# VectorE's evictions ahead of the ranks, and two expert pairs' rows kept on the chip, in a decoder layer with sparse attention and 32 experts

## The chip, the cores and the metric

The program runs on one core of a Trainium2 chip. The metric is the device time of one execution in microseconds (us), lower is better. Everything is float32; the large projections outside the experts run as three passes over operands split into a rounded part and its rest.

## The reference, cut to what matters

One layer over 512 tokens of width 1024: a projection, sparse attention beside causal pooling, an output projection, a layer norm, and then a layer of experts with a second layer norm. Only the last part matters here:

```python
pg_top, g = lax.top_k(softmax(t @ w_r1 + b_r1), 1)          # one of 4 groups
pe, e_local = lax.top_k(softmax((t @ w_r2 + b_r2)[group g]), 2)   # two of its 8 experts
weights = pg_top * pe / sum(pe)
for e in range(32):
    a = silu(t @ w_gate[e]) * (t @ w_up[e])                 # 1024 -> 256
    y = y + combine[:, e:e + 1] * (a @ w_down[e])           # 256 -> 1024
out = layer_norm(ALPHA * t + y)
```

Each token goes to two of the 32 experts. One expert's weights are 3 MB, all of them 96 MB, and each is read once.

## The kernel before, in words

**Up to the router.** The 512 tokens are 4 tiles of 128. For each tile TensorE (PE) makes the output projection, VectorE (DVE) adds the residual and takes the statistics, ScalarE (ACT) normalises, PE transposes the normalised rows (`transpose_h`, L1377), ACT evicts four of the eight 128x128 blocks (L829) and DVE the other four (`transposed_h`, L1048), and PE multiplies them with the router's weights (`router`, L1386). Meanwhile GpSimd (POOL) scales the tile with the norm's gain and offset (L683, L684), and SyncE (SP) stores it to `h_rows` in HBM. DVE's `route` (L1055 to L1078) finds the group and the two experts of each token.

**Ranks and lists.** A token's place among those of its expert is a rank: PE multiplies a triangle with the one-hot rows (`ranks`, L1408, L1409), DVE's `place` (L1102 to L1111) turns the ranks of several tiles into one-hot rows over 64 places (`at_rank`, L1107), and PE multiplies these with the token numbers (`lists`, L1416). Tiles 0 to 2 are ranked together, and tile 3 by itself once its `route` is done. DVE's order of work is as it is written in the code: `place` for tiles 0 to 2, `transposed_h(3)`, `route(3)`, `place` for tile 3, the lists (`row_from`, L1122).

**The pairs.** Two experts of 64 places each make a pair, 16 pairs in all (p = 0 to 15, `LAST` = 15). POOL gathers a pair's 128 rows from HBM (`gather`, L698, into `xe`), PE transposes them (`rows`, L1446), PE multiplies with gate and up weights (`gate_up`, L1460, 32 matmuls), ACT and DVE make the activation (L852, L1129), PE transposes it (L1471) and multiplies with the down weights (`down`, L1484, 16 matmuls). DVE and ACT evict the halves of the result into `ye` (`y_out`, L1135, L865), one buffer, and POOL scatters the rows to `y_rows` in HBM (`store_y`, L705), for pairs 0 to 14. An eviction of pair p waits until the store of p-1 has landed. The weights go through six slots, three pairs' worth. SP issues all of them on its one queue: a pair's gate and up weights when the pair three before is through `gate_up`, its down weights when that pair is through `down`.

**The end.** When pair 13 is through `down`, SP loads gain and offset of the second norm (`g2`, `b2`, L549, L550). Then it waits until all 15 stores have landed and reads `y_rows` back in eight loads of 512 KB, two for each tile (`yg`, L563). Between them stands a branch for the case that an expert has more than 64 tokens (L554, not taken here). Pair 15 is not stored: DVE builds for each tile of tokens a matrix of weights (`place_w`, L1170, 8 instructions, after pair 13), PE transposes it (L1539) ahead of pair 15's `gate_up`, ACT evicts it (`placeT`, L902), and PE multiplies it with pair 15's rows (L1548, 8 products of two instructions), so that the rows come out at their tokens. On DVE the end is `add_stored(0)` (two instructions, L1209), `gated(15)` (L1129), `add_stored(1)`, `add_stored(2)`, `y_out(15)`, `add_stored(3)`, and then for each tile `add_last` (L1216 to L1220) and `finish` (L1225, L1226).

Of the kernel before, what the change touches and what calls it, by code (L numbers as in the profile page):

```python
# [30 lines left out]
ALU = mybir.AluOpType  # L31
# [3 lines left out]
P = 128  # L35
# [25 lines left out]
LAST = PAIRS - 1  # L61
PAIR_SLOTS = ((2, 3), (1, 0), (4, 5))
# [26 lines left out]
def layer_kernel(nc, x, w_in, w_pool, pool_scale, w_out, rel_bias, ln1_g, ln1_b, w_r1, b_r1, w_r2, b_r2,  # L89
                 w_gate, w_up, w_down, ln2_g, ln2_b, onehot, headfix, out):  # L90
    ctx = ExitStack()
    with ctx:
# [13 lines left out]
        for j in range(SLOTS):  # L106
# [38 lines left out]
        place_w = at("place_w", SLOT + 20 * KB, [NT, 2, CAP])  # L145
        placeT = at("placeT", SLOT + 22 * KB, [NT, P])
# [20 lines left out]
        ye = at("ye", o, [D])  # L167
# [7 lines left out]
                   [at("x_again1_0", o + 4 * KB, [D // 2]), at("x_again1_1", o + 10 * KB, [D // 2])]]  # L175
        sil = [at(f"sil{i}", o + 4 * KB + KB * i, [DE]) for i in range(2)]
# [68 lines left out]
        last_rank, last_wt = at("last_rank", wpool_at, [2, NT, 2]), at("last_wt", wpool_at + 64, [2, NT, 2])  # L245
        row_sum, neg_mean = at("row_sum", wpool_at + 128, [NT, 2]), at("neg_mean", wpool_at + 160, [NT])
        square_sum, std2, rstd2 = [at(name, wpool_at + 192 + 32 * i, [NT]) for i, name in enumerate(("square_sum", "std2", "rstd2"))]
# [119 lines left out]
        y_stored = sem("y_stored")  # L367
# [72 lines left out]
        LAST_BANKS = ((0, 1), (2, 3), (6, 7), (4, 5))  # L440
# [5 lines left out]
        def _(sp):  # L446
# [104 lines left out]

            sp.wait_ge(y_ps, 2 * LAST)
# [6 lines left out]

            sp.wait_ge(y_stored, 16 * LAST)  # L560
            for t in range(NT):
                for c in range(2):
                    sp.dma_start(yg[t][c][:, :], y_dram[SEQ * c + P * t:SEQ * c + P * t + P, :]).then_inc(y_gathered[t], 16)  # L563
# [9 lines left out]
        def _(pool):  # L573
# [128 lines left out]
            def store_y(p):  # L702
                pool.wait_ge(y_lo, p + 1)
                pool.wait_ge(y_hi, p + 1)
                pool.indirect_dma_start(out=y_dram, out_offset=bass.IndirectOffsetOnAxis(ap=row_to[:, p:p + 1], axis=0),  # L705
                                        in_=ye[:, :], in_offset=None,
                                        bounds_check=2 * SEQ - 1, oob_is_err=False).then_inc(y_stored, 16)
# [5 lines left out]
            for p in range(LAST):  # L713
                if p + 3 < PAIRS:
                    gather(p + 3)
                store_y(p)
# [3 lines left out]
        def _(act):  # L720
# [140 lines left out]
            def y_out(p):  # L861
                act.wait_ge(y_ps, 2 * p + 2)
                if p:
                    act.wait_ge(y_stored, 16 * p)
                act.activation(ye[:, 512:], bank[5][:, :], ACT.Copy).then_inc(y_hi, 1)  # L865
# [15 lines left out]
            for p in range(LAST - 1):  # L881
                rows_out(p + 2)
                silu(p + 1)
                y_out(p)
                act_out(p + 1)
            y_out(LAST - 1)

# [13 lines left out]
            act.wait_ge(placeT_ps, 1)  # L901
            act.activation(placeT[:, :, :], bank[0][:, :].rearrange("p (t s) -> p t s", t=NT), ACT.Copy).then_inc(placeT_ready, 1)  # L902
            silu(LAST)
            act_out(LAST)
            y_out(LAST)
            for t in range(NT):
# [7 lines left out]
        def _(dve):  # L914
# [216 lines left out]
            def y_out(p):  # L1131
                dve.wait_ge(y_ps, 2 * p + 1)
                if p:
                    dve.wait_ge(y_stored, 16 * p)
                dve.tensor_copy(ye[:, 0:512], bank[4][:, :]).then_inc(y_lo, 1)  # L1135
# [21 lines left out]
            for c in range(2):  # L1157
                link(dve.tensor_tensor(last_rank[:, c, :, :], hot[:, :, c, NE - 2:NE], rk[:, :, c:c + 1].to_broadcast([P, NT, 2]), ALU.mult))
                link(dve.tensor_tensor(last_wt[:, c, :, :], hot[:, :, c, NE - 2:NE], wt[:, :, c:c + 1].to_broadcast([P, NT, 2]), ALU.mult))
# [3 lines left out]
            for p in range(LAST - 1):  # L1163
                rows_out(p + 2)
                gated(p + 1)
                y_out(p)

            for t in range(NT):
                for e in range(2):
                    ins = dve.tensor_scalar(place_w[:, t, e, :], iota_r[:, :], last_rank[:, 0, t, e:e + 1], last_wt[:, 0, t, e:e + 1],  # L1170
                                            ALU.is_equal, ALU.mult)
            ins.then_inc(place_ready, 1)
# [71 lines left out]
        def _(pe):  # L1244
# [247 lines left out]
            for p in range(LAST - 1):  # L1492
                rows(p + 2)
                gate_up(p + 1)
                down(p)
                transpose_act(p + 1)
# [37 lines left out]

            pe.wait_ge(xeT_act, PAIRS)
            pe.wait_ge(xeT_dve, PAIRS)
            pe.wait_ge(place_ready, 1)
            for t in range(NT):
                ins = pe.transpose(bank[0][:, P * t:P * t + P], place_w[:, t, :, :].rearrange("p n s -> p (n s)"), ident[:, :])  # L1539
            ins.then_inc(placeT_ps, 1)  # L1540
# [3 lines left out]
            pe.wait_ge(placeT_ready, 1)  # L1544
            for t in range(NT):
                for c in range(2):
                    pe.wait_ge((y_lo, y_hi)[c], PAIRS)
                    pe.matmul(bank[LAST_BANKS[t][c]][:, :], placeT[:, t, :], ye[:, 512 * c:512 * c + 512], start=True, stop=True).then_inc(last_ps, 1)  # L1548

# [25 lines left out]
```

## Time and profile before

| | us |
|---|---|
| the three runs | 616.8, 593.65, 613.6 |
| their median | 613.6 |
| the profiled execution | 593.69 |
| its span | 592.0 |
| PE busy | 499.4 (84%) |
| DVE busy | 229.1 (39%) |
| POOL busy | 161.9 (27%) |
| ACT busy | 149.7 (25%) |

The span runs from the first to the last instruction; 1.7 us of the profiled execution lie around it. Times within the trace are microseconds from the span's start. Busy shares are means over stages with different limits, so that a term is read from the waits of its own stage. A clock of 1.00 in the rows is TensorE at 2.4 GHz, 0.50 at 1.2 GHz. The profiled execution lies at the lowest of the three runs, 20 us below their median.

### The profile page before, as it was taken

Reading aid. Unit: us, or ns where it says so; the run is one execution under the profiler, and the core shown is the slowest. Engines: PE = TensorE matmul, PEld = TensorE weight load, DVE = VectorE, ACT = ScalarE, POOL = GpSimd, SP = SyncE. Lnnn points to the kernel's source line nnn. Section 1 sums busy time; section 2 is a strip of 40 time slices with the busy share of each in tenths; the row PEclk is TensorE's granted clock in tenths of the full one; section 3 lists DMA queues with packets and bytes.
Section 4 is the critical chain, followed back from the end, with each engine's and each line's share of the span. In section 5 each row is a group of like instructions: output and inputs, shape, how many; then the busy total and the mean of one; then the engine's idle time right before and its main releaser. Section 6 shows DMA issues by size and latency. Waiting matters only on the chain.

```text
span 592.0 us, 6141 instructions
## 1 busy us (share of the span) xinstructions
PE 499.4 (84%) x2182; PEld 283.7 (48%) x2182; DVE 229.1 (39%) x554; ACT 149.7 (25%) x311; POOL 161.9 (27%) x159
## 2 busy tenths in 40 slices
PE   5999999999799999999547799999786789777490
PEld 4586675856454556888443333333232333332130
DVE  2101482898789751255740211111111110102287
ACT  3233323522246664012410111111111111011032
POOL 2243332387624762033521011211111110101000
PEclk9999999999899999999757899999799998889875
DMA  9844458103029101990757799999999999998613
GB/s 321 298 50 51 51 164 259 38 1 142 1 92 356 52 1 37 389 389 38 276 222 270 303 396 418 422 417 419 421 421 419 422 419 419 422 420 329 237 78 142
DMA packets 42583, 148.29 MB, mean 251 GB/s; under 512 B 11362, under 2 KB 15970, under 8 KB 30264
## 3 DMA queue, kind: packets, MB, share of 16 engines
q1 hardware_dynamic: 37992, 139.71, 62.5%
q0 software_dynamic: 4464, 8.10, 3.7%
q8 instruction: 18, 0.29, 0.2%
q14 instruction: 13, 0.11, 0.1%
q10 hardware_dynamic: 96, 0.08, 0.0%
HBM read 137.16 MB, written 18.87 MB: 264 GB/s over the span
## 4 chain that ended last, share of the span: by engine, by line
PE 54%; DMA 20%; SPq 9%; DVE 7%; issue 5%; POOL 2%; ACT 2%; POOLq 0%; DVEq 0%; ACTq 0%
PE bank L1295 17%; DMA wgu<-in_w_up_dram 10%; PE bank L1460 8%; PE bank L1400 7%; DMA xe<-h_rows,row_from 6%; SPq L486 6%; PE bank L1268 3%; PE bank L1484 3%; PE bank L1362 3%; PE bank L1340 3%; SPq L489 3%; DMA y_rows<-ye,row_to 2%; PE bank L1315 2%; PE bank L1353 2%; PE bank L1446 1%
## 5 line engine op out<-in xcount | busy, mean ns | idle before, releaser
L1460 PE MATMUL bank<-wgu,xeT 128*64 128x512 f32 x512 | 127.9, 657 | 28.0 <-DMA wgu<-in_w_up_dram 27.2
L1460 PEld LDWEIGHTS bank<-wgu,xeT 128*64 128x64 f32 x512 | 42.6, 151 | 102.3 <-issue 100.1
L705 POOL DMA_INDIRECT y_rows<-ye,row_to x15 | 15.1, 1006 | 189.0 <-PE bank L1446 120.0
L1484 PE MATMUL bank<-wd,actT 128*64 128x512 f32 x256 | 60.7, 617 | 1.4 <-ACT actT L859 1.4
L1129 DVE TENSOR_TENSOR act_row<-bank,sil 128x256 f32<-128x256 f32 x16 | 6.8, 425 | 130.3 <-ACT sil L852 130.3
L607 POOL TENSOR_TENSOR ring_low<-ring,wt_high 128x1024 fp32r<-128x1024 f32 x12 | 28.6, 2384 | 55.4 <-ACT wt_high L732 55.4
L852 ACT ACTIVATE sil<-bank 128x256 f32<-128x256 f32 x16 | 6.1, 384 | 138.7 <-PE bank L1460 138.7
L1484 PEld LDWEIGHTS bank<-wd,actT 128*64 128x64 f32 x256 | 20.6, 142 | 37.6 <-issue 37.6
L1295 PE MATMUL bank<-xT_high,ring_low 128*128 128x512 f32 x128 | 32.7, 397 | 0.0
L1143 DVE COPY xeT<-bank 128x512 f32<-128x512 f32 x16 | 11.1, 692 | 54.6 <-PE bank L1446 54.6
L1340 PE MATMUL bank<-kT,qT 64*128 64x128 f32 (+3 forms) x64 | 26.0, 487 | 5.1 <-DVE nmx L995 4.3
L955 DVE SCALAR_TENSOR_TENSOR score<-relu,iw,score 128x256 f32<-128x256 f32 (+2 forms) x21 | 19.8, 942 | 26.2 <-ACT relu L775 26.0
L670 POOL TENSOR_SCALAR lg<-lg,rinv 128x128 f32<-128x128 f32 (+3 forms) x32 | 19.3, 603 | 34.8 <-DVE rinv L1025 34.8
L1295 PE MATMUL bank<-xT_high,wt_high 128*128 128x512 f32 (+1 forms) x104 | 28.1, 415 | 0.0
L937 DVE MAX8 m<-score 128x8 f32<-128x256 f32 (+2 forms) x48 | 26.9, 561 | 2.7 <-POOL score L641 1.6
L1295 PEld LDWEIGHTS bank<-xT_high,ring_low 128*128 128x128 f32 x128 | 23.4, 188 | 8.7 <-issue 3.6
L1295 PE MATMUL bank<-xT_low,wt_high 128*128 128x512 f32 (+1 forms) x104 | 27.3, 406 | 0.0
L1446 PE MATMUL bank<-ident,xe 128*128 128x128 f32 x128 | 19.4, 299 | 8.9 <-DMA xe<-h_rows,row_from 8.9
L1400 PE MATMUL bank<-wo_high,mix_high 128*128 128x512 f32 x64 | 25.5, 398 | 1.5 <-issue 1.5
L938 DVE MATCH_REPLACE8 score<-m,score 128x256 f32<-128x256 f32 (+2 forms) x48 | 26.1, 543 | 0.0
L1400 PE MATMUL bank<-wo_low,mix_high 128*128 128x512 f32 x64 | 25.0, 390 | 0.0
L1400 PE MATMUL bank<-wo_high,mix_low 128*128 128x512 f32 x64 | 24.9, 389 | 0.0
(202 smaller groups left out, 761.8 us busy)
## 6 DMA issues: line engine op xcount, KB each, us to landing
wgu<-in_w_gate_dram SPq DMA_DIRECT2D x32, 1024.0 KB, 23.2
wgu<-in_w_up_dram SPq DMA_DIRECT2D x32, 1024.0 KB, 27.7
wd<-in_w_down_dram SPq DMA_DIRECT2D x32, 1024.0 KB, 28.5
ring<-in_w_in_dram SPq DMA_DIRECT2D x5, 2048.0 KB, 13.1
wo<-in_w_out_dram SPq DMA_DIRECT2D x2, 2048.0 KB, 7.9
y_rows<-zero SPq DMA_DIRECT2D x1, 4096.0 KB, 21.8
yg<-y_rows SPq DMA_DIRECT2D x8, 512.0 KB, 6.6
bias_rows<-brow SPq DMA_DIRECT2D x1, 2560.0 KB
```

The source lines that it names most:

```text
L486: sp.dma_start(wgu[j][:, s, :, :], src[0, bass.ds(e, 1), :, :].rearrange("o (p k) f -> p (o k) f", p=P)).then_inc(loaded, 16)
L607: pool.tensor_tensor(low, raw, high.bitcast(F32), ALU.subtract).then_inc(wt_low_ready, 1)
L670: pool.tensor_scalar(p, p, rinv[:, u % 8:u % 8 + 1], 1.0, ALU.mult, ALU.mult).then_inc(prob_ready, 1)
L937: link(dve.max(m8[:, :], s_b))
L938: link(dve.match_replace(out=s_b, in_to_replace=m8[:, :], in_values=s_b, imm_value=TAKEN))
L955: ins = dve.scalar_tensor_tensor(out=s_b, in0=r, scalar=iw[:, b, j:j + 1], in1=s_b, op0=ALU.mult, op1=ALU.add)
L1295: ins = pe.matmul(bank[2 + i % 2][0:rows_out, :], lhsT, rhs, start=(s, k) == (0, 0), stop=(s, k) == (2, KD - 1))
L1340: pe.matmul(bank[qk_bank(u)][:, 0:keys(b)], qT[half(hh), hh // 2, P * b:P * b + P], kT[half(hh), hh // 2, 0:keys(b)], start=True, stop=Tru ...
L1400: ins = pe.matmul(bank[(2 if t % 2 == 0 else 0) + i][:, :], lhsT, rhs, start=(k, s) == (0, 0), stop=(k, s) == (KD - 1, 2))
L1446: ins = pe.transpose(bank[k // 4][:, P * (k % 4):P * (k % 4) + P], xv[:, k, :], ident[:, :])
L1460: ins = pe.matmul(bank[2 + i][half_rows(n), :], xeT[i][:, k, half_rows(n)], wgu[slots[n]][:, :, k, :], start=k == 0, stop=k == KD - 1)
L1484: ins = pe.matmul(bank[4 + c][half_rows(n), :], actT[i][:, m, half_rows(n)], wd[PAIR_SLOTS[p % 3][n]][:, m, 512 * c:512 * c + 512], start= ...
```

## The change

Two things are done.

1. In DVE's code `transposed_h(3)` stands ahead of `place` for tiles 0 to 2.
2. Pairs 14 and 15 (`KEPT` = 2) are both kept on the chip, and pairs 0 to 13 (`STORED` = 14) are stored. `ye` has two buffers, used in turn, each with its own semaphore, and an eviction waits for the store of two pairs before. The placing matrices for the two kept pairs are built in the loop's rounds 4 and 5 (`PLACE` = 4): DVE's 8 instructions at the round's start, PE's 4 transposes after `down`, into bank 6 or 7, and ACT's copy after its `act_out`. SP issues the eight `yg` loads ahead of the branch, when the stores of pairs 0 to 13 have landed. PE multiplies pair 14's rows for tiles 0 and 1 ahead of pair 15's `gate_up` and adds pair 15's to them afterwards; for tiles 2 and 3 both pairs' products come after `down(15)`. ACT computes one square root of one element after `y_out(15)`, which loads the table for it ahead of the norm's.

```diff
             sp.dma_start(b2[:, :], ln2_b[0].partition_broadcast(P)).then_inc(ln2_in, 16)
+            for i in range(2):
+                sp.wait_ge(y_stored[i], 16 * (STORED // 2))
+            for t in range(NT):
+                for c in range(2):
+                    sp.dma_start(yg[t][c][:, :], ...).then_inc(y_gathered[t], 16)
+
             sp.wait_ge(y_ps, 2 * LAST)
...
-            sp.wait_ge(y_stored, 16 * LAST)
-            for t in range(NT):
-                for c in range(2):
-                    sp.dma_start(yg[t][c][:, :], ...).then_inc(y_gathered[t], 16)
...
             def y_out(p):
                 dve.wait_ge(y_ps, 2 * p + 1)
-                if p:
-                    dve.wait_ge(y_stored, 16 * p)
-                dve.tensor_copy(ye[:, 0:512], bank[4][:, :]).then_inc(y_lo, 1)
+                if p >= 2:
+                    dve.wait_ge(y_stored[p % 2], 16 * (p // 2))
+                dve.tensor_copy(ye[p % 2][:, 0:512], bank[4][:, :]).then_inc(y_lo, 1)
...
+            transposed_h(NT - 1)
             dve.wait_ge(rank_ps, 1)
             place(0, NT - 1, bank[3][:, 0:NE * (NT - 1)])
-            transposed_h(NT - 1)
             route(NT - 1)
...
             for p in range(LAST - 1):
+                if 0 <= p - PLACE < KEPT:
+                    q = p - PLACE
+                    if q:
+                        dve.wait_ge(placeT_ps, q)
+                    for t in range(NT):
+                        for e in range(2):
+                            ins = dve.tensor_scalar(place_w[:, t, e, :], iota_r[:, :], ...)
+                    ins.then_inc(place_ready, 1)
                 rows_out(p + 2)
...
                 down(p)
+                if 0 <= p - PLACE < KEPT:
+                    pe.wait_ge(place_ready, p - PLACE + 1)
+                    for t in range(NT):
+                        ins = pe.transpose(bank[6 + p % 2][:, P * t:P * t + P], place_w[:, t, :, :]..., ident[:, :])
+                    ins.then_inc(placeT_ps, 1)
+                if 0 <= p - PLACE - 1 < KEPT:
+                    pe.wait_ge(placeT_ready, p - PLACE)
                 transpose_act(p + 1)
...
+            for t in range(2):
+                place_rows(t, STORED)
             gate_up(LAST)
             transpose_act(LAST)
             down(LAST)
+            for t in range(2):
+                place_rows(t, LAST)
+            for t in range(2, NT):
+                place_rows(t, STORED)
+                place_rows(t, LAST)
```

On DVE, between the router of tile 2 and that of tile 3, the order before is this (`hT_134` is the eviction of tile 3's transposes, `gl` the first instruction of `route(3)`):

```order
L1078 TENSOR_SCALAR neg<-em_191 128x1
L1102 SCALAR_TENSOR_TENSOR hot_rank<-bank,hot 128x3x32 x2
L1105 TENSOR_REDUCE rk<-hot_rank 128x6
L1107 TENSOR_TENSOR at_rank<-iota_r,rk 128x128 x3
L1111 TENSOR_TENSOR rank_219<-hot_rank 128x96
L1048 TENSOR_SCALAR hT_134<-bank,gT,bT 128x128 x4
L1055 TENSOR_TENSOR gl<-bank,br 128x4
```

The same place after the change:

```order
L1084 TENSOR_SCALAR neg<-em_192 128x1
L1054 TENSOR_SCALAR hT_132<-bank,gT,bT 128x128 x4
L1108 SCALAR_TENSOR_TENSOR hot_rank<-bank,hot 128x3x32 x2
L1111 TENSOR_REDUCE rk<-hot_rank 128x6
L1113 TENSOR_TENSOR at_rank<-iota_r,rk 128x128 x3
L1117 TENSOR_TENSOR rank_220<-hot_rank 128x96
L1061 TENSOR_TENSOR gl<-bank,br 128x4
```

The four evictions have moved ahead of the seven instructions of `place`; `route(3)` follows the last of these instead of the evictions.

On SP, at the program's end, the loads of `yg` stood behind the branch and ahead of the output's stores:

```order
L489 DMA wd_58<-in_w_down_dram 128x2048
L555 REGISTER_ALU
L555 COMPARE_AND_BRANCH
L554 UNCONDITIONAL_BRANCH
L563 DMA yg_0_100<-y_rows 128x1024
L563 DMA yg_1_101<-y_rows 128x1024
```

After the change they follow the norm's gain and offset directly:

```order
L492 DMA wd_56<-in_w_down_dram 128x2048
L552 DMA g_108<-in_ln_g_dram 128x1024
L553 DMA b_109<-in_ln_b_dram 128x1024
L559 DMA yg_0_100<-y_rows 128x1024
L559 DMA yg_1_101<-y_rows 128x1024
L559 DMA yg_0_102<-y_rows 128x1024
L559 DMA yg_1_103<-y_rows 128x1024
```

What has moved is the eight loads, past the wait for pair 14's `down` and past the branch. `wd_56` is the last load of expert weights, so nothing but gain and offset stands between the weights and `yg` on SP's queue.

## Rows read from the trace of the kernel before

**Rows 1.** The page: DMA busy tenths in 40 slices of 14.8 us.

```profile
DMA  9844458103029101990757799999999999998613
```

**Rows 2.** Windows: us, busy PE, PEld, DVE, ACT, POOL, clock, DMA share, GB/s.

```profile
304.00:309.00 5.00, 2.10 (x14) 1.89 (x14) 3.07 (x18) 2.06 (x5) 0.00 (x0) 0.50 0.00 0
520.00:535.00 15.00, 11.20 (x46) 4.38 (x48) 1.78 (x4) 0.53 (x2) 1.01 (x1) 0.89 1.01 419
549.00:553.00 4.00, 4.00 (x22) 1.41 (x18) 0.00 (x0) 0.00 (x0) 0.00 (x0) 1.00 0.13 45
```

**Rows 3.** Chain that ended last, 289 to 352 us: start, us, what.

```profile
289.57 1.98 PE bank L1377 x8
...
293.09 5.43 issue
298.52 3.62 PE bank L1386 x16
...
308.29 0.18 DVE row_from L1122
...
309.42 4.20 DMA xe<-h_rows,row_from
...
344.25 7.02 PE bank L1460 x32
```

**Rows 4.** Timeline of DVE, 292 to 302 us.

```profile
292.54 0.42 DVE L1102 SCALAR_TENSOR_TENSOR hot_rank<-bank,hot 128x96 f32<-128x96 f32 x2 [0.77 <-PE bank L1409]
...
293.38 3.35 DVE L1107 TENSOR_TENSOR at_rank<-iota_r,rk 128x128 f32<-128x128 f32 x3
...
297.06 1.36 DVE L1048 TENSOR_SCALAR hT<-bank,gT,bT 128x128 f32<-128x128 f32 x4
```

**Rows 5.** The first three at_rank instructions: ns min/median/max, first and last start.

```profile
L1107 DVE TENSOR_TENSOR at_rank<-iota_r,rk x3: 277/803/2425, 293.4 to 294.3; 128x128 f32<-128x128 f32 x3
```

**Rows 6.** Timeline of POOL, 284 to 320 us.

```profile
294.12 2.47 POOL L684 TENSOR_TENSOR h<-h,b 128x1024 f32<-128x1024 f32 x1
```

**Rows 7.** Tile h_rows, its store issued by SP at 296 to 297 us.

```profile
DMA to landing us min/median/max: 5.5/5.5/5.5
```

**Rows 8.** Line L1170, which builds the placing matrices on DVE.

```profile
L1170 DVE TENSOR_SCALAR place_w<-iota_r,last_rank,last_wt x8: 306/315/317, 534.9 to 536.5; 128x64 f32<-128x64 f32 x8
```

**Rows 9.** Timeline of PE, 536 to 576 us.

```profile
540.76 0.66 PE L1539 MATMUL bank<-ident,place_w 128*128 128x128 f32 x4
...
544.83 8.67 PE L1460 MATMUL bank<-wgu,xeT 128*64 128x512 f32 x32 [3.41 <-DMA wgu<-in_w_up_dram]
...
569.23 7.13 PE L1548 MATMUL bank<-ye,placeT 128*128 128x512 f32 x16
```

**Rows 10.** Chain that ended last, 532 to 569 us.

```profile
532.58 3.45 PE bank L1484 x16
...
537.51 7.85 DMA y_rows<-ye,row_to
...
553.78 4.54 DMA yg<-y_rows
...
560.98 0.43 DVE act_row L1129
...
562.84 6.46 PE bank L1484 x16
```

**Rows 11.** Line L550: the second norm's offset, issued at 536.4 us.

```profile
DMA to landing us min/median/max: 16.5/16.5/16.5
```

**Rows 12.** Tile yg, the last two loads, issued at 556.6 and 557.1 us.

```profile
DMA to landing us min/median/max: 8.1/8.5/8.9
```

**Rows 13.** Timeline of DVE, 560 to 575 us.

```profile
561.32 5.24 DVE L1209 SCALAR_TENSOR_TENSOR h<-yg,wt,h 128x1024 f32<-128x1024 f32 x4
...
567.22 2.60 DVE L1209 SCALAR_TENSOR_TENSOR h<-yg,wt,h 128x1024 f32<-128x1024 f32 x2
570.53 0.69 DVE L1216 CUSTOM_DVE_ANT_0 h<-bank,h 128x512 f32<-128x512 f32 x1 [0.72 <-PE bank L1548]
```

More of the change, by code:

```diff
@@ L61 @@
 LAST = PAIRS - 1
+KEPT = 2
+STORED = PAIRS - KEPT
+PLACE = 4
 PAIR_SLOTS = ((2, 3), (1, 0), (4, 5))
@@ L166, in layer_kernel @@
         hT = [at(f"hT{i}", o + 4 * KB * i, [KD, P]) for i in range(2)]
-        ye = at("ye", o, [D])
+        ye = [at(f"ye{i}", o + 4 * KB * i, [D]) for i in range(2)]
         o += 8 * KB
@@ L244, in layer_kernel @@
         eps_t = small("eps_t", [1])
[L245 to L247 removed]
+        last_rank, last_wt = at("last_rank", wpool_at, [2, NT, 2 * KEPT]), at("last_wt", wpool_at + 128, [2, NT, 2 * KEPT])
+        row_sum, neg_mean = at("row_sum", wpool_at + 256, [NT, 2]), at("neg_mean", wpool_at + 288, [NT])
+        square_sum, std2, rstd2 = [at(name, wpool_at + 320 + 32 * i, [NT]) for i, name in enumerate(("square_sum", "std2", "rstd2"))]
         rank1 = small("rank1", [NT, NE])
@@ L366, in layer_kernel @@
         y_hi = sem("y_hi")
-        y_stored = sem("y_stored")
+        y_stored = [sem(f"y_stored{i}") for i in range(2)]
         y_gathered = [sem(f"y_gathered{t}") for t in range(NT)]
@@ L712, in _ @@
             pool.wait_ge(y_zeroed, 16)
-            for p in range(LAST):
+            for p in range(STORED):
                 if p + 3 < PAIRS:
@@ L862, in y_out @@
                 act.wait_ge(y_ps, 2 * p + 2)
-                if p:
-                    act.wait_ge(y_stored, 16 * p)
-                act.activation(ye[:, 512:], bank[5][:, :], ACT.Copy).then_inc(y_hi, 1)
+                if p >= 2:
+                    act.wait_ge(y_stored[p % 2], 16 * (p // 2))
+                act.activation(ye[p % 2][:, 512:], bank[5][:, :], ACT.Copy).then_inc(y_hi, 1)
             for t in range(NT):
@@ L885, in _ @@
                 act_out(p + 1)
+                if 0 <= p - PLACE < KEPT:
+                    act.wait_ge(placeT_ps, p - PLACE + 1)
+                    act.activation(placeT[:, p - PLACE, :, :], bank[6 + p % 2][:, :].rearrange("p (t s) -> p t s", t=NT), ACT.Copy).then_inc(placeT_ready, 1)
             y_out(LAST - 1)
@@ L905, in _ @@
             y_out(LAST)
+            act.activation(probe[:, :], eps_t[:, :], ACT.Sqrt)
             for t in range(NT):
@@ L1166, in _ @@
                 y_out(p)
[L1168 to L1172, printed above, removed]
             y_out(LAST - 1)
@@ L1533, in _, with place_rows @@
                         ins.then_inc(o_y_ps, 1)
+                pe.wait_ge(o_added, NE * NT + 1)
+            def place_rows(t, p):
+                for c in range(2):
+                    pe.wait_ge((y_lo, y_hi)[c], p + 1)
+                    ins = pe.matmul(bank[LAST_BANKS[t][c]][:, :], placeT[:, p - STORED, t, :], ye[p % 2][:, 512 * c:512 * c + 512],
+                                    start=p == STORED, stop=p == LAST)
+                    if p == LAST:
+                        ins.then_inc(last_ps, 1)
             pe.wait_ge(xeT_act, PAIRS)
             pe.wait_ge(xeT_dve, PAIRS)
[L1537 to L1540, printed above, removed]
+            for t in range(2):
+                place_rows(t, STORED)
             gate_up(LAST)
```

29 lines of the change are left out of this document (13 added, 16 removed).

## The prediction, made before the changed kernel ran

> **What bounds the kernel now.** I read the page's slices first: the DMA engines are at nine tenths or more in an unbroken run of slices from the 24th to the 36th, 340 to 533 us, with an idle patch before it and a falling tail behind [rows 1]. The windows say the same in numbers: share 1.01 and 419 GB/s in 520 to 535 us, nothing at all in 304 to 309 us, and 0.13 in 549 to 553 us [rows 2]. So the expert stage is as long as its weights take, and what can be won lies before it, where nothing streams because the first gather isn't out, and behind it. The chain of waits, read in order of time, names both places: in the first, the router of tile 3 and the lists [rows 3]; in the second, pair 13's store, the first loads of `yg`, and pair 15's last matmuls [rows 10]. The timelines of single engines then tell what stands in each wait [rows 4 to 6, 9, 13].
>
> **Part 1, the eviction of tile 3 ahead of the ranks.** PE ends tile 3's transposes at 289.57 + 1.98 = 291.55 us. ACT's half follows at once: its eviction ends where the chain's 5.43 us of "issue" begin, at 293.09. DVE's half comes only after `place`, at 297.06 to 298.42 [rows 4], and the router starts at 298.52 [rows 3]. Now DVE evicts first. It is free at about 291.8 (the end of tile 2's route, just before its wait for the ranks ended at 292.54 [rows 4]), so with 1.36 us the eviction ends at 293.2, beside ACT's. The router runs 293.3 to 296.9, with the same 3.62 us.
>
> `route(3)`, which started when the router ended (298.52 + 3.62 = 302.14), now has two things to wait for: the router at 296.9, and `place`, which has moved behind the eviction. `place` starts at 293.2, and `at_rank` 0.84 us later (293.38 less 292.54 [rows 4]), at 294.0. Its three instructions took 277, 803 and 2425 ns [rows 5]: the third started at 294.3, under POOL's addition of 294.12 to 296.59 [rows 6], and ended right behind it. I take it that what is left of `at_rank` is held until 296.59 again, then takes two times 0.28 us, and 0.26 us of `rank` follows: 297.5. So `route(3)` starts at 297.6 and wins 302.1 - 297.6 = **4.5 us**. Bounds: 5.3 us if nothing is held and the router alone decides (302.1 - 296.9); 3.6 us if the three take their whole 3.35 us again from 294.0 with a wait of a microsecond behind. A loss is excluded: POOL's addition ends at 296.6 whatever DVE does.
>
> The Trainium skill (GPSIMD Engine Reference, Specifications) states that GpSimd shares SBUF interfaces with VectorE and that DVE instructions with two SBUF inputs contend for them. This case's trace agrees: 2425 ns against 277 for one shape. By the rule the term is 4.5 us, without it 5.3 us; the evictions, which read PSUM, keep their 1.36 us by it.
>
> Does the 4.5 us reach the end? The lists' last step moves from 308.5 to 304.0, and the gather needs `h_rows` as well: tile 3's store is issued when POOL's addition ends, at 296.6, and lands 5.5 us later, at 302.1 [rows 7]. That is 1.9 us early, so it doesn't decide. The next weights wait for the first gather, and the DMA engines are empty meanwhile [rows 2]; from the gather on [rows 3] every load is issued in a fixed chain behind it. The idle patch is cut by what is won, and the saturated stage of equal bytes moves as a whole. I count all 4.5 us.
>
> **Part 2, the placing work in rounds 4 and 5.** In each of the two rounds 8 instructions of 0.31 us on DVE, 2.5 us [rows 8], 4 transposes of together 0.66 us on PE [rows 9] and one copy on ACT; one such set goes at the end. I cost it at nothing. Its cover is the stream: PE runs ahead of it at this point, since three pairs were loaded early, and later waits for each pair's weights (3.41 us for the last [rows 9]). Without the cover a round would cost its 2.5 + 0.66 us, plus the price of a `gate_up` after a stall: 8.67 us against 7.02 us without one [rows 3, 9].
>
> **Part 3, the end.** Gone: pair 14's store (its issue on POOL and its landing), and the wait of `y_out(14)` for pair 13's store. PE's four products for pair 14 go in front of pair 15's `gate_up`. Eight such products took 7.13 us [rows 9], four take 3.6, from 541.4 (540.76 + 0.66) to 545.0, where PE waited for weights until 544.83 [rows 9]. Cost at most 0.2 us, and hidden, as shown below. They also keep PE at work, so `gate_up(15)` may run at 2.4 GHz throughout, 7.0 instead of 8.67 us.
>
> What matters is when `yg` for tile 0 has landed, since on DVE `add_stored(0)` stands ahead of `gated(15)`, and PE stood still from 553.5 until that was done, at 561.4 [rows 10]. Before, the loads were issued when pair 14's store had landed, 0.4 us ahead of the chain's 553.78, and tile 0 landed at 558.3, 4.9 us after that issue [rows 10]. Now they are issued when pair 13's store has landed, 537.51 + 7.85 = 545.4. Taken alone that is 8 us earlier. But the DMA engines aren't empty then. The norm's offset, the last thing on SP's queue ahead of `yg`, was issued at 536.4 and landed only at 552.9, 16.5 us later [rows 11], while the mean share had fallen to 0.13 [rows 2]: a few of the 16 engines still worked off weights when the others had nothing to do. A load is spread over all 16 and has landed with the slowest. So tile 0's `yg` ends behind the offset on the slowest engine: 552.9 plus two loads' shares. In the kernel before the second of the eight loads landed at 558.3 and the eighth at 566.0 (557.1 + 8.9 [rows 12]), 1.3 us apart, so 552.9 + 2.6 = 555.5. The term is 558.3 - 555.5 = **2.8 us**. Bounds: 1.6 us if the slow engine keeps the pace of its last two loads (3.8 us for the pair); 8.6 us if it doesn't hold up `yg` at all (next part).
>
> Behind that, all goes as before and 2.8 us earlier: PE has stood still, so `down(15)` takes its 6.46 us again, against 3.45 us for the same work in pair 13 [rows 10], as at half the clock [rows 10]; `add_stored(1)`, `(2)`, `y_out(15)` and `add_stored(3)` take 5.24 + 0.7 (567.22 less 566.56) + 2.6 us on DVE [rows 13] beside it. Four products come on top for tiles 2 and 3, 3.6 us, but DVE works from 570.5 to the end of the span on the four tiles, 5 us a tile, while PE was through at 576.4 [rows 9, 13]: hidden. The square root's table isn't on the path, since DVE first uses its result after the second tile's `add_last`.
>
> The Trainium skill (DMA: Bandwidth & Descriptors, Queues, rings and completion order) says that each DMA engine consumes the descriptors of a queue in ring order. That speaks against the early issue, and the offset's 16.5 us agree. By the rule the term is 2.8 us, without it 8.6 us.
>
> **Sum.** 593.7 - 4.5 - 2.8 = **586.4 us** for an execution like the profiled one. That one is the lowest of those shown, the median is 613.6 us, 20 us above, and nothing in the profile tells where these 20 us lie; I take the difference as the same there: 613.6 - 7.3 = **606.3 us**, 1.2% less.
>
> **The rivals.**
> *The loads aren't held up.* If `yg` for tile 0 lands 4.9 us after its issue as before, at 550.3 in the trace's time, `add_stored(0)` is done at 552.9. `gate_up(15)`, without a fall of the clock, ends at 552.0, so `gated(15)` runs at 552.9, `down` stays at 2.4 GHz (3.45 instead of 6.46 us [rows 10]), and DVE's own work decides: 553.3 + 5.2 + 0.7 + 2.6 = 561.9 instead of 570.5 [rows 13]. That is 8.6 us, with part 1 13.1 us: 580.6, at the median 600.5 us. For it: the bytes left at 549 us are few [rows 2]. Against: the offset's landing.
> *The stream swallows part 1.* If some DMA engines are so far behind that they never run dry between 304 and 340 us, the last weights come no earlier: only 2.8 us are left, 590.9, at the median 610.8 us. Against: the share is 0.00 for 5 us [rows 2].
> *Rounds 4 and 5 cost time: slower.* DVE builds the matrices ahead of `rows_out`, and PE waits for them between `down` and the next transposes. If PE decides there, each round costs 2.5 + 0.66 + 1.65 us (the last for the clock), 9.6 us for both, less the 7.3: 596.0, at the median 615.9 us, 2.3 us slower than before. For it: PE is nearly fully busy in this part of the stage. Against: the stream is saturated to 535 us [rows 2], and DVE's work fits while PE ends `down`. It decides from the point where the DMA share falls below 1 after these rounds.
>
> **How the numbers follow.** Forecast 0.60, loads not held up 0.18, part 1 swallowed 0.12, rounds cost time 0.10. The range must hold executions like the lowest and like the highest of those shown: down to 593.7 - 5.3 - 8.6 = 579.8, up to 616.8 - 3.6 - 1.6 = 611.6 us: 580 to 612. Two per cent, about what a measurement of this kernel can tell from no change, are 12 us. Only the first rival reaches that (13.1), so faster by more than 2% is 0.19 with a little for scatter; slower by more than 2% is 0.04, for scatter; within 2% 0.77.
>
> **What would show it.** Right: the router of tile 3 starting near 293.3 and the first gather 4.5 us earlier; the last `gate_up`'s weights at about 540.3; `yg` for tile 0 landing some 10 us after its issue, not 5; DMA share 1.0 through rounds 4 and 5. Wrong: `at_rank` ending after 298.5; pair 15's `down` at 3.5 us; a gap in the DMA share around pairs 4 to 7; tile 0's `yg` waited for by nobody.

## The result, and the profile after

| | before | after |
|---|---|---|
| the runs of this comparison, us | 616.8, 593.65, 613.6, 594.0 | 584.9, 584.92, 607.5, 586.08 |
| median | 603.8 | 585.5 |
| profiled execution | 593.69 | 584.9 |
| its span | 592.0 | 583.1 |

The ratio is 0.9865, with an interval of 0.9835 to 0.9895: 8 us less of 594. It isn't the ratio of the medians, because some executions of either kernel are 20 us longer (in the traces of e1_order and e11_twelve below, which are such executions, the granted clock is 0.50 from 200 to 240 us, where the profile after has 1.00), and the ratio leaves these out. The forecast was 7.3 us less, 586.4 for an execution like the profiled one. The changed kernel run once more gave 0.9864.

The page's slices (14.6 us each) answer to [rows 1]:

```profile
DMA  9944468004019200892487799999999999999803
```

The unbroken run of nines goes from 335 to 539 us, where it went from 340 to 533. The tail behind it was 8, 6 and 1 tenths, then 3 for the output's stores. Now it is 8 and 0, then 3: the eight `yg` loads fill the slice right behind the weights, where a few engines used to work alone.

Three windows of the changed kernel, with the columns of [rows 2]. The second holds PE's and ACT's placing work of rounds 4 and 5 and DVE's of round 5, the third is the stage behind it:

```profile
298.00:303.00 5.00, 2.11 (x14) 1.89 (x14) 3.28 (x19) 2.06 (x5) 0.00 (x0) 0.50 1.00 418
388.00:404.00 16.00, 15.56 (x84) 6.91 (x80) 4.14 (x12) 4.10 (x9) 2.82 (x3) 1.00 1.02 419
404.00:420.00 16.00, 14.49 (x72) 5.71 (x72) 2.50 (x4) 2.16 (x5) 3.27 (x4) 1.00 1.02 421
```

Before, 5 us ahead of the first gather had share 0.00 [rows 2]; now the early loads of weights run until 303, and the gather is issued at 303.69. Of the idle patch ahead of the gather some 0.7 us are left. Behind the gather a second one stands as before, where the next weights wait for `gate_up`: share 0.00 in 338 to 340 us before, in 332 to 334 us after. Through the placing rounds the share stays above 1.

The chain of waits of the changed kernel, 291 to 308 us (start, us, what), answers to [rows 3]:

```profile
291.16 1.36 DVE hT L1054 x4
292.53 0.34 DVE hot_rank L1108 x2
292.89 0.36 DVE rk L1111
293.28 2.86 DVE at_rank L1113 x3
...
296.27 0.26 DVE rank L1117
296.53 0.08 DVE gl L1061
...
302.57 0.19 DVE row_from L1128
...
303.69 4.45 DMA xe<-h_rows,row_from
```

The 5.43 us of "issue" and PE's router are gone from it. DVE evicts, makes the ranks and goes straight into `route(3)`. `row_from` stands at 302.57 instead of 308.29, 5.72 us earlier. Of that, 0.83 us were won before this place: tile 3's transposes start at 288.74 against 289.57, and nothing that the change touches lies ahead of them. It is scatter: in e12_again, the same kernel once more, they start at 290.18. So part 1 gave 4.9 us. From tile 3's transposes to `row_from` it is 18.72 us before and 18.71 in e2_kept, which has the old order; it is 13.83 us after and in e1_order and 13.82 in e12_again, which have the new one.

The three instructions that decide when `route(3)` starts are in the timelines of PE, of DVE's `at_rank` (ns min/median/max, first and last start) and of POOL:

```profile
292.63 3.60 PE L1395 MATMUL bank<-wr,hT 128*128 128x36 f32 x16 [0.96 <-ACT hT L833]
```

```profile
L1113 DVE TENSOR_TENSOR at_rank<-iota_r,rk x3: 279/293/2437, 293.3 to 295.8; 128x128 f32<-128x128 f32 x3
```

```profile
293.28 2.49 POOL L688 TENSOR_TENSOR h<-h,b 128x1024 f32<-128x1024 f32 x1
```

PE's wait is put down to ACT, but ACT's eviction is done at 292.25 and DVE's at 292.52, so DVE's is the one that releases the router, at 292.63. The router ends at 296.23 and `place` at 296.53, within 0.3 us. Again one `at_rank` takes 2.44 us beside POOL's addition, by itself in DVE's timeline:

```profile
293.49 2.44 DVE L1113 TENSOR_TENSOR at_rank<-iota_r,rk 128x128 f32<-128x128 f32 x1
```

This time it is the second: the first starts with the addition at 293.28 and takes its 0.29 us. The second ends at 295.93, 0.16 us behind the addition (295.77), and the third takes 0.28 us again.

The end, from the chain of waits of the changed kernel, answers to [rows 10]:

```profile
532.10 7.94 DMA y_rows<-ye,row_to
540.08 0.05 issue
540.13 0.33 SPq L559
540.46 0.04 issue
540.50 8.86 DMA yg<-y_rows
...
552.03 0.44 DVE act_row L1135
...
553.89 6.62 PE bank L1493 x16
```

And the offset's landing, which answers to [rows 11]; it was issued at 531.0:

```profile
DMA to landing us min/median/max: 15.8/15.8/15.8
```

`yg` is issued when pair 13's store has landed, and tile 0 lands at 549.36, 8.95 us earlier than before. The last weights that PE waits for, pair 15's up weights, came 5.33 us earlier (539.50 against 544.83), so part 2's and 3's own share is 3.6 us. It repeats: tile 0 lands 13.5 us behind these weights before and 13.6 in e1_order, and 9.9 after, 10.0 in e2_kept and 10.2 in e12_again, a share of 3.3 to 3.7 us.

PE's timeline, with the end of [rows 9]:

```profile
535.36 3.70 PE L1557 MATMUL bank<-ye,placeT 128*128 128x512 f32 x8
539.50 7.09 PE L1469 MATMUL bank<-wgu,xeT 128*64 128x512 f32 x32 [0.44 <-DMA wgu<-in_w_up_dram]
552.51 0.70 PE L1480 MATMUL bank<-ident,act_row 128*128 128x128 f32 x2 [5.92 <-DVE act_row L1135]
553.89 6.62 PE L1493 MATMUL bank<-wd,actT 128*64 128x512 f32 x16 [0.68 <-ACT actT L863]
560.44 10.57 PE L1557 MATMUL bank<-ye,placeT 128*128 128x512 f32 x24
```

Pair 14's four products end 0.44 us before the last weights are there and cost nothing. With PE at work until then, `gate_up(15)` takes 7.09 us instead of 8.67. That gain is worth nothing, since PE then waits 5.92 us for DVE, which waits for `yg`. `down(15)` is as slow as before, 6.62 us. The first `add_last` starts at 561.74 against 570.53 [rows 13].

### The profile page after: what moved, and what is told of

Same layout as the page of the kernel before. It is cut to its first block, busy times and chain, and to the rows that moved or that the text cites. A ratio compares the mean times of both kernels' runs of the same rounds, so it can differ in the third digit from the quotient of the medians.

```text
span 583.1 us, 6186 instructions
## 1 busy us (share of the span) xinstructions
PE 505.0 (87%) x2202; PEld 286.7 (49%) x2202; DVE 229.5 (39%) x562; ACT 150.5 (26%) x313; POOL 161.2 (28%) x158
## 4 chain that ended last, share of the span: by engine, by line
PE 54%; SPq 15%; DMA 13%; DVE 9%; issue 4%; POOL 2%; ACT 2%; POOLq 0%; DVEq 0%; ACTq 0%
PE bank L1304 17%; SPq L489 10%; PE bank L1469 8%; PE bank L1409 8%; DMA wgu<-in_w_up_dram 5%; SPq L492 5%; DMA xe<-h_rows,row_from 4%; PE bank L1493 3%; PE bank L1277 3%; PE bank L1371 3%; PE bank L1349 3%; PE bank L1324 2%; PE bank L1455 2%; PE bank L1362 2%; DMA yg<-y_rows 2%
## 5 line engine op out<-in xcount | busy, mean ns | idle before, releaser
L1469 PE MATMUL bank<-wgu,xeT 128*64 128x512 f32 x512 | 126.4, 650 | 23.3 <-DMA wgu<-in_w_up_dram 22.5
```

Of the source, the lines that this page charges most:

```text
L1469: ins = pe.matmul(bank[2 + i][half_rows(n), :], xeT[i][:, k, half_rows(n)], wgu[slots[n]][:, :, k, :], start=k == 0, stop=k == KD - 1)
```

## The experiments

Each kernel is compared with the kernel before on the same chip. "Of before" and "of after" say which kernel an edit starts from. Line numbers of edited kernels differ by one or two.

### The two halves by themselves

e1_order, of before:

```diff
+            transposed_h(NT - 1)
             dve.wait_ge(rank_ps, 1)
             place(0, NT - 1, bank[3][:, 0:NE * (NT - 1)])
-            transposed_h(NT - 1)
             route(NT - 1)
```

> The kernel before with part 1 alone: DVE evicts tile 3's transposes ahead of place for tiles 0 to 2. Theory: the 4.9 us that the two traces differ by between tile 3's transposes and the lists come from this alone, and the weights' stream behind it moves as a whole, so the last gate_up's weights land 4.9 us earlier and the time falls by 4.9 us (0.8%), from 593.7 to 588.8. The tail stays: tile 0's stored rows land 17 us after pair 15's last up weights are waited for, as before. Rival (the stream swallows it): the first gather comes 5 us earlier, but the last weights at the same time, 593.7.

Measured: 0.9917 (0.9903 to 0.9932), 4.9 us less. In its trace the distance from `row_from` to the last weights is 236.7 us, as it is before (236.5) and after (236.9). The stage isn't always as regular: it is 237.9 us in e12_again and 238.1 in e2_kept. So what is won ahead of the first gather passes through the streamed stage, to within this spread of 1.6 us; the ratio says the same with 0.9 us either way.

e2_kept, of after: the same lines put back into the order before, so that pairs 14 and 15 are kept and nothing else is changed.

> Part 2 alone: two kept pairs and early loads, the eviction back behind the ranks. Theory: only the tail gains, 3.6 us (what the stored rows of tile 0 came earlier by, counted from the last weights): 590.1 from 593.7. Place and route as in the kernel before (route of tile 3 starts 10.6 us after PE's transposes end). Rival (the two parts need each other, or rounds 4 and 5 cost something that part 1 hides): less than 2 us, 592 or more.

Measured: 0.9933 (0.9915 to 0.9952), 4.0 us less. The two halves add up to 8.9 us; the whole gave 8.0, known to 1.8 us either way: they are additive within what can be told. PE's timeline of this kernel:

```profile
540.20 3.70 PE L1557 MATMUL bank<-ye,placeT 128*128 128x512 f32 x8
545.97 8.78 PE L1469 MATMUL bank<-wgu,xeT 128*64 128x512 f32 x32 [2.06 <-DMA wgu<-in_w_up_dram]
```

Here a wait of 2.06 us was enough for a slow `gate_up(15)`, 8.78 us, where the changed kernel's 0.44 us left it at 7.09. The time of the whole doesn't show it.

### What holds up the yg loads

The prediction said that they queue behind the offset on the slowest DMA engines. A rival says that what counts is the ring that they stand in, so that another queue frees them; another that `yg` is slow by itself at this place.

e3_behind, of after, lets SP issue gain and offset behind `yg`:

```diff
-            sp.dma_start(g2[:, :], ln2_g[0].partition_broadcast(P)).then_inc(ln2_in, 16)
-            sp.dma_start(b2[:, :], ln2_b[0].partition_broadcast(P)).then_inc(ln2_in, 16)
-
...
             for t in range(NT):
                 for c in range(2):
                     sp.dma_start(yg[t][c][:, :], ...).then_inc(y_gathered[t], 16)
+            sp.dma_start(g2[:, :], ln2_g[0].partition_broadcast(P)).then_inc(ln2_in, 16)
+            sp.dma_start(b2[:, :], ln2_b[0].partition_broadcast(P)).then_inc(ln2_in, 16)
```

> The changed kernel with the loads of the second norm's gain and offset (g2, b2) behind the eight yg loads on SP's queue instead of ahead of them. Theory (yg is held on the slowest DMA engine by what stands ahead of it in the queue, of which g2 and b2 are the last 2.5 to 3.8 us): yg for tile 0 lands 5.5 to 6.5 us after its issue instead of 9.2, gated(15) about 2.5 to 3.5 us earlier, and the time falls from 584.9 to about 582. Rival (yg is slow by itself, by eight reads at once or by rows just written): it lands 9 us after its issue again, and the time is 584.9. Second rival: gain and offset now land so late that the last adds wait for them, 586 or more.

Measured: 0.9787 (0.9769 to 0.9806), 581.4 to 583.0 us. From its chain of waits:

```profile
541.18 6.50 DMA yg<-y_rows
```

Tile 0 lands 6.9 us after the issue at 540.81, not 9.2: a little later than expected, with the time as expected. By the ratios this is 4.6 us less than the changed kernel, by the two profiled spans 1.8 (581.3 against 583.1). Its last weights came at 540.30, so `yg` landed 7.4 us behind them. In the changed kernel the offset landed 7.3 us behind them (546.8 less 539.5). `yg` has taken the offset's place. The second rival fell too: gain and offset are there at 557.7, 2.1 us ahead of the first `add_last` at 559.85.

e4_actq, of after, lets ACT's queue issue the eight loads, gain and offset staying on SP's:

```diff
-                    sp.dma_start(yg[t][c][:, :], ...).then_inc(y_gathered[t], 16)
...
+                    act.dma_start(yg[t][c][:, :], ...).then_inc(y_gathered[t], 16)
```

> The changed kernel with the eight yg loads issued by ScalarE on its own DMA queue, at the same moment (both store semaphores complete, after y_out(14)); SP's queue holds weights, gain and offset as before. Theory (ring order within a queue holds yg, and each engine shares its time between two queues): yg for tile 0 lands about 5 to 6 us after its issue instead of 9.2, and the time is about 581 to 582; the last down weights land up to 3 us later, hidden. Rival (the slowest engine, or the reads themselves, are slow whatever the queue): 9 us again, 584.9.

Measured: 583.3, 583.6, 606.5 and 606.9 us; there is no ratio. From its chain, and the offset's landing:

```profile
540.39 8.66 DMA yg<-y_rows
```

```profile
DMA to landing us min/median/max: 18.7/18.7/18.7
```

The expectation fell. Issued at 540.0 from a queue of its own, tile 0 still landed at 549.05, 9.1 us later. The offset, which nobody had moved, landed at 549.7 instead of 546.8. The last weights came at 539.5 in both kernels. So the two queues aren't independent: what the one gets, the other loses. The Trainium skill says why (DMA: Bandwidth & Descriptors, Issuing engines are not separate DMA queues): DMAs of different engines run on the same 16 DMA engines and interleave. The offset's 2.9 us agree. Of the two rules on that page of the Trainium skill, ring order (which the prediction cited) and this one, it is this one that tells what another queue is worth. The time is still some 1.5 us below the changed kernel's. `yg` is 0.3 us earlier, and `down(15)` took 5.04 us instead of 6.62, so that the first `add_last` didn't wait for PE, as it does for 0.88 us in the changed kernel: 1.2 us together. The 0.88 us don't come from the queue, since the changed kernel run once more (e12_again) hasn't got them either:

```profile
556.57 4.96 PE L1493 MATMUL bank<-wd,actT 128*64 128x512 f32 x16 [0.67 <-ACT actT L863]
```

Why PE's clock rises earlier in one execution than in the other stays open.

e10_late, of after, makes the issue of `yg` wait for the offset as well:

```diff
             for i in range(2):
                 sp.wait_ge(y_stored[i], 16 * (STORED // 2))
+            sp.wait_ge(ln2_in, 32)
```

> The changed kernel, but SP issues the yg loads only when gain and offset have landed (one more wait on SP), about 546.8 instead of 540.1. Theory (yg is held by the work left on the slowest engine, so the 6.7 us of waiting there cost little): tile 0's rows land 4.9 us after that issue, at 551.7 instead of 549.4, and the time rises by 2.3 us to 587.2. Rival (yg takes 9 us by itself when eight loads are issued at once): 556, and the time rises by 6 to 7 us.

Measured: 0.9889 (0.987 to 0.9908), 586.9 and 588.4 us. From the chain:

```profile
531.64 15.71 DMA b<-in_ln_b_dram
547.82 4.55 DMA yg<-y_rows
```

Tile 0 lands at 552.37, 4.9 us after an issue at 547.45, the 4.9 us of before [rows 10]. So `yg` isn't slow by itself, and what is still under way at its issue is what makes it 9.2. The trace keeps the time of each semaphore count, and the two loads of tile 0 give 32 of them. In e10_late all 32 are in 4.9 us after the issue. In the changed kernel 28 are in after the same 4.9 us, at 545.05, and the last four come at 547.1, 548.1, 548.4 and 549.4. So most of the load isn't held up at all, and a few late parts of it set the landing. The run also says what the early issue is worth: issued 7.3 us earlier, the loads land 3.0 us earlier, and the time is 1.4 us less by the two ratios, 2.1 by the two profiled spans (2.3 expected).

### Whether the placing rounds are covered

e5_place0 and e6_place11 set `PLACE` of after to 0, the first rounds, and to 11, the last possible.

```diff
-PLACE = 4
+PLACE = 0
```

> The changed kernel with the placing matrices built in rounds 0 and 1 instead of 4 and 5 (PLACE = 0). In round 0 and 1 the DMA engines still wait for PE (the next weights are issued when gate_up of a pair ends), so the work has no cover. Theory: DVE's 8 instructions (2.5 us) stand ahead of rows_out in a chain that decides, so each round costs some 1 to 3 us and the time is 2 to 5 us above the changed kernel, 587 to 590. Rival (the placing work is hidden in any round, since DVE is idle two thirds of the stage): 584.9.

Measured: 0.985 (0.9833 to 0.9867), 584.3 to 586.0 us. The loss that was expected isn't there. DVE's timeline of e5_place0:

```profile
325.51 0.42 DVE L1135 TENSOR_TENSOR act_row<-bank,sil 128x256 f32<-128x256 f32 x1
325.85 1.87 DVE L1176 TENSOR_SCALAR place_w<-iota_r,last_rank,last_wt 128x64 f32<-128x64 f32 x8
327.63 0.68 DVE L1149 COPY xeT<-bank 128x512 f32<-128x512 f32 x1
```

The eight instructions lie behind the activation that PE waits for and ahead of an eviction for the pair after next, which PE needs a round later. So even in the first rounds, where the stream isn't unbroken yet (DMA share 0.78 and 0.79 in 315 to 345 us), 1.9 us of DVE find room. There the order of DVE's work is the likely cover; no run separates it from DVE's idle time.

> The changed kernel with the placing matrices built in rounds 11 and 12 (PLACE = 11), where PE waits for weights in every pair. Theory: rounds 4 and 5 cost nothing, so moving the work changes nothing, 584.9. Rival (rounds 4 and 5 do cost, as PE is nearly full there): 1 to 8 us less than the changed kernel.

Measured: 0.9861 (0.984 to 0.9882). No difference, as expected.

e11_twelve, of after, builds the matrices twelve times over, so that each of the two rounds has 96 instructions where it had 8; the repeats write the same values again:

```diff
-                    for t in range(NT):
-                        for e in range(2):
-                            ins = dve.tensor_scalar(place_w[:, t, e, :], ...)
+                    for rep in range(12):
+                        for t in range(NT):
+                            for e in range(2):
+                                ins = dve.tensor_scalar(place_w[:, t, e, :], ...)
```

> The changed kernel with DVE's eight instructions for the placing matrix made twelve times over in each of rounds 4 and 5 (some 22 us of DVE a round instead of 1.9; the same values are written again). A round of PE is 12.4 us there, so PE is kept waiting about 8 to 10 us in each of the two rounds. Theory (the stream is the cover: weights stand in the DMA queue for 23 to 28 us, and a late PE issues the next ones late without letting the engines run dry): at most 2 us more than the changed kernel, below 587. Rival (what covers is only DVE's idle time within a round, and the stream breaks off when PE is late): 8 to 18 us more, 593 to 603.

Measured: 0.9849 (0.9834 to 0.9865), 584.6 to 585.8 us: no cost. Its DVE, its PE, and its windows with the columns of [rows 2]:

```profile
396.74 23.01 DVE L1177 TENSOR_SCALAR place_w<-iota_r,last_rank,last_wt 128x64 f32<-128x64 f32 x96
```

```profile
419.81 1.12 PE L1511 MATMUL bank<-ident,place_w 128*128 128x128 f32 x4 [6.42 <-DVE place_w L1177]
...
444.20 1.11 PE L1511 MATMUL bank<-ident,place_w 128*128 128x128 f32 x4 [9.77 <-DVE place_w L1177]
```

```profile
410.00:420.00 10.00, 3.58 (x17) 1.04 (x14) 9.82 (x42) 0.98 (x2) 0.00 (x0) 0.90 1.02 424
430.00:440.00 10.00, 4.43 (x22) 1.24 (x18) 9.82 (x43) 0.98 (x2) 0.00 (x0) 0.92 1.02 422
440.00:450.00 10.00, 5.80 (x24) 3.68 (x26) 6.29 (x22) 1.45 (x3) 2.03 (x2) 0.57 1.02 424
450.00:460.00 10.00, 10.00 (x54) 3.89 (x50) 1.16 (x3) 1.74 (x4) 0.00 (x0) 1.00 0.84 331
```

PE stood still for 6.42 and then 9.77 us, waiting for `place_w`, and the mean clock of 440 to 450 us is 0.57. The weights kept coming at a share of 1.02 during the stalls. In 450 to 460 us the share dips to 0.84, since SP issues the next weights only at 455.2 us, when the late `gate_up` has ended. Even those 1.6 us can't be seen in the time; they are no more than the spread of the streamed stage (236.5 to 238.1 us), and here it took at most 237.6. This shows the cover: PE's lead over the stream took in stalls of 16.2 us together, and the rival in which the two rounds cost 9.6 us had no ground.

### DVE's order at the end

e7_gated, of after, puts `gated(15)` ahead of `add_stored(0)`, so that PE doesn't wait for `yg`:

```diff
-            add_stored(0)
             gated(LAST)
+            add_stored(0)
```

> The changed kernel with gated(15) ahead of add_stored(0) on DVE, so that pair 15's activation doesn't wait for tile 0's stored rows. Theory: PE's down(15) starts about 548 instead of 553.9 us and stays at 2.4 GHz (3.5 us instead of 6.6), but DVE's own work behind the arrival of tile 0's rows (eight adds of 1.3 us and an eviction, 11.1 us from 549.4) then decides: the first add_last at 560.5 instead of 561.7, 1.2 us less, 583.7. Rival (PE's late start is what the end waits for): the whole 6 to 9 us, 576 to 579.

Measured: 0.9842 (0.9822 to 0.9863), 584.0 to 584.8 us. PE's and DVE's timelines:

```profile
549.10 3.65 PE L1493 MATMUL bank<-wd,actT 128*64 128x512 f32 x16 [0.68 <-ACT actT L863]
558.53 13.20 PE L1557 MATMUL bank<-ye,placeT 128*128 128x512 f32 x24 [5.78 <-DVE ye L1141]
```

```profile
549.86 7.89 DVE L1218 SCALAR_TENSOR_TENSOR h<-yg,wt,h 128x1024 f32<-128x1024 f32 x6 [2.00 <-DMA yg<-y_rows]
557.79 0.69 DVE L1141 COPY ye<-bank 128x512 f32<-128x512 f32 x1
...
561.02 0.69 DVE L1225 CUSTOM_DVE_ANT_0 h<-bank,h 128x512 f32<-128x512 f32 x1
```

`down(15)` runs at full clock, 3.65 us, and is over at 552.8. The 7.8 us that PE wins are worth 0.7: the first `add_last` moves from 561.74 to 561.02, with `yg` 0.5 us later here. What stands between `yg`'s landing and that step is DVE's own work, eight additions of 1.31 us and one eviction, whatever PE does. Most of it is lost again one step later. PE stood still for 5.78 us ahead of its products and makes them in 13.20 us instead of 10.57, the second `add_last` waits 0.74 us for them, and the span is 583.0 us against 583.1.

e8_both, of after, is the edits of e3_behind and e7_gated together.

> gated(15) ahead of add_stored(0) and g2, b2 behind the yg loads, both. Theory: tile 0's rows arrive at about 546.0, gated(15) at 547.0, and DVE's work decides: first add_last at about 557.5, 4 us less than in the changed kernel, 581 us. Alone the two give about 3 and 1.2 us. Rival: if yg isn't moved by its place in the queue, 583.7 as with gated(15) alone.

Measured: 0.982 (0.98 to 0.9839), 581.9 to 583.4 us, no better than e3_behind alone (spans 580.7 and 581.3). Its PE:

```profile
556.40 12.26 PE L1556 MATMUL bank<-ye,placeT 128*128 128x512 f32 x24 [3.69 <-DVE ye L1140]
```

`y_out(15)` stands behind the third addition on DVE, so PE waits 3.69 us for pair 15's rows, starts its products slowly, and the second `add_last` waits 0.56 us for them.

e9_tail, of e8_both, moves that eviction one tile forward:

```diff
             add_stored(1)
-            add_stored(2)
             y_out(LAST)
+            add_stored(2)
             add_stored(3)
```

> As with gated(15) first and g2, b2 behind yg, and DVE evicts pair 15's first half (y_out) after add_stored(1) instead of after add_stored(2). With both edits alone PE stood still for 3.7 us before the placing products and began them at 1.2 GHz, and add_last(0) waited 0.6 us for them. Theory: y_out at about 553, PE goes on without a gap at 2.4 GHz, the wait is gone and DVE works without a pause from 547.4 us: 0.5 us less than both edits alone, about 582.0 (span 580.3). Rival (the placing products decide the end and not DVE's work): 2 to 4 us less.

Measured: 0.9795 (0.9781 to 0.9809), 581.5 to 583.2 us, span 580.2, the 0.5 us below e8_both that were expected. PE and DVE:

```profile
553.76 10.57 PE L1556 MATMUL bank<-ye,placeT 128*128 128x512 f32 x24 [1.05 <-DVE ye L1140]
```

```profile
547.74 5.24 DVE L1217 SCALAR_TENSOR_TENSOR h<-yg,wt,h 128x1024 f32<-128x1024 f32 x4
553.01 0.69 DVE L1140 COPY ye<-bank 128x512 f32<-128x512 f32 x1
553.62 5.24 DVE L1217 SCALAR_TENSOR_TENSOR h<-yg,wt,h 128x1024 f32<-128x1024 f32 x4
558.89 0.69 DVE L1224 CUSTOM_DVE_ANT_0 h<-bank,h 128x512 f32<-128x512 f32 x1
```

From 547.4 us on, when tile 0 has landed, DVE has no pause up to the first `add_last`. `gated(15)` starts at that same moment, behind `gate_up(15)`, so in this order a still earlier `yg` would win nothing ahead of it. With e3_behind this is the best version: some 12 us below before (0.9795 and 0.9787, their intervals overlap) and some 4 below after.

e12_again is the changed kernel once more, in the same series as e9_tail to e11_twelve.

> The changed kernel itself once more, beside the others on this chip: 584.9, ratio to the kernel before 0.9865.

Measured: 0.9864 (0.9846 to 0.9883), as in the first comparison.

## Why the prediction was right, and where its numbers were off

**Part 1: right, 4.9 us instead of 4.5.** The steps are there: DVE's eviction beside ACT's (it ends 0.27 us behind it), POOL's addition holding one `at_rank` to its own end, `place` and the router ending almost together. The difference is in `at_rank`: one short instruction stood behind the held one, where two were reckoned, as the first had got through. `route(3)` was reckoned for 297.6, which is 296.8 after taking off the 0.83 us won earlier; it came at 296.5. That the gain reaches the end is shown by e1_order's ratio, 4.9 us with 0.9 either way, and by the distances from the lists to the last weights, 236.5 to 238.1 us in five traces. The prediction's reason, an idle patch on the DMA engines, is right and has a limit that it didn't state: the patch ahead of the gather is now nearly gone, so that the gather of a further gain of this kind would meet the early loads (not tried).

**Part 2: right at nothing, with the wrong idea of where the cover ends.** The work was also over-counted: eight instructions on DVE overlap and take 1.9 us, not 2.5. In rounds 4 and 5 the stream covers it: e11_twelve puts 23 us on DVE into each round and loses nothing that shows. In the expectation of e5_place0 I took it that in the first rounds the cover would be missing; e5_place0 shows that it isn't; that DVE evicts a pair's rows a round before they are needed is the likely reason.

**Part 3: right in its mechanism, 3.6 us instead of 2.8.** The mis-sized term is the offset's landing. I left it where it was, at 552.9, 8.1 us behind the last weights. It landed 7.3 us behind them, 0.7 us earlier by that measure. Pair 14's store fits as the reason: with it the offset lands 8.1 us behind the weights (before, e1_order), without it 7.3 to 7.7 (after, e2_kept, e12_again). The step from there to tile 0's `yg` was put at 2.6 us and took 2.5. The rival without a hold-up (8.6 us) is refuted by the 9.2 us to the landing, against 4.9 in e10_late.

The rule of the Trainium skill that was cited for it (DMA: Bandwidth & Descriptors, Queues, rings and completion order), ring order within a queue, told less than the number. Order does matter, as e3_behind shows. But e4_actq shows that leaving the queue buys at most 0.3 us. What holds the loads up is the work that the slowest DMA engines still have, from all queues together. The semaphore counts under e10_late bear this out: four of tile 0's 32 counts are late and the rest aren't.

**The sum.** 4.9 + 3.6 us, and 0.8 us that were there before the place of the change, make 9.3 us. Of these 8.9 show in the span, since the last weights came 0.4 us later behind the lists; by the ratio it is 8.0. The two parts were put 0.4 and 0.8 us too low, and the 0.8 us of scatter are luck and no part of the change. The absolute 606.3 us took over the median of the three runs before, 20 us above the profiled one; the median after is 585.5. The range of 580 to 612 us was as wide as these runs made it and would have held no change as well: what tests the account is the two terms, not the range.

**The rivals.** Part 1 wasn't swallowed. Rounds 4 and 5 cost nothing. The point from which they would decide was given as a DMA share below 1 after them. With twelve times the work it was reached, 0.84 over 10 us, and still nothing shows in the time. Neither product nor clock mattered on PE: `gate_up(15)` became 1.6 us shorter, and that went into PE's wait for DVE.

## What to carry to other kernels

At the end of a saturated stream the mean DMA share can fall long before the last load is in. So count the place of a load from the end of the stream, put the loads that are waited for ahead of those that aren't (e3_behind), and don't count on another queue (e4_actq). Ahead of such a stage what is won came through in full here, behind it only what DVE's own work let through. Inside it even 10 us of a waiting PE may count for nothing, which a kernel with multiplied work shows in one run.

## What the runs showed of the hardware that was not expected

- **A few late parts hold a whole load.** Issued into the tail of the stream, tile 0's loads had 28 of 32 semaphore counts in after 4.9 us, the time that all 32 took once the tail was through (e10_late), and the last four 2.0 to 4.3 us later.
- **A second queue takes from the first.** With `yg` on ACT's queue, the offset on SP's landed 18.7 us after its issue instead of 15.8, and `yg` 9.1 instead of 9.2 (e4_actq).
- **A short break of the stream doesn't show.** Two stalls of PE of 6.4 and 9.8 us, and a dip of the DMA share to 0.84 over 10 us, left no trace in the time (e11_twelve).
- **An instruction of DVE that starts under POOL's is held to the end of POOL's.** Before, it was the third `at_rank` (2.43 us), after, the second (2.44 us), each ending 0.15 us behind POOL's addition, against 0.28 us for those that weren't held. One that started within 0.01 us of the addition got through. The 0.80 us of the first `at_rank` before are of the same kind: it ended 0.14 us behind POOL's multiplication (294.04). The Trainium skill (GPSIMD Engine Reference, Specifications) names the shared interfaces; the size of the hold, the rest of POOL's instruction, is this trace's.
- **The price of a stop of PE isn't fixed by its length.** `gate_up(15)` took 7.09 us after a wait of 0.44 us and 8.78 after 2.06 us; `down(15)` took 3.65 us after waits of 0.93 and 0.68 us. But behind a long wait for `act_row` and 0.68 us more, `down(15)` took 6.62 us (5.92 us of waiting, after), 4.96 (6.27 us, e12_again) and 5.30 (8.31 us, e10_late). Where DVE decides, as at this kernel's end, these differences are worth less than a microsecond.
